# Overflow blocks, token sums and final norm moved into the block of the expert loop

## The reference

```python
x = x + g1 * mix
h2 = rmsnorm(x, norm2) * (1.0 + sc2) + sh2
ffn = moe(h2, ...)            # top 4 of 32 experts; 1024 -> 1024 (gate, up) -> 1024 (down)
x = x + g2 * ffn
y = rmsnorm(x, final_norm)
# moe: contrib = y_rows[dest] * g_s[:, None];  zeros_like(h).at[tok_s].add(contrib)
```

## Time and profile before

| | us |
|---|---|
| median of 3 runs | 1440.04 (1436.89 to 1440.72) |
| the profiled execution's own time | 1436.63 |
| its span | 1434.8 |
| PE busy | 1278.8 (89% of the span) |
| DVE, ACT, POOL busy | 459.5, 135.3, 282.2 |
| data moved by DMA | 479.23 MB, 334 GB/s over the span |

### The profile page before, as it was taken

How to read it: one execution, slowest core, us unless ns; L and a number is a source line. 1 busy time by engine, 2 the same in 40 slices (tenths; PEclk the granted TensorE clock), 3 DMA queues, 4 the chain that set the end, 5 groups by cost and what they waited for, 6 DMA issues and landing times. The chain is left out here.

```text
span 1434.8 us, 32026 instructions
## 1 busy us (share of the span) xinstructions
PE 1278.8 (89%) x13745; PEld 746.7 (52%) x13745; DVE 459.5 (32%) x676; ACT 135.3 (9%) x270; POOL 282.2 (20%) x335
## 2 busy tenths in 40 slices
PE   4999989566999999999999999999999999999710
PEld 2777634311356556655555665544545666566500
DVE  1210153452222333322223333222233333222244
ACT  3100101200000000100000000100000001000102
POOL 4002100152111111222111111221111112220126
PEclk9999989779999999999999999999999999999955
DMA  9736830625999999999999999999999999999161
GB/s 325 223 111 230 329 145 30 257 101 198 398 417 409 412 413 410 409 398 395 419 416 411 405 412 410 406 406 416 409 412 408 411 407 396 414 405 415 44 260 68
DMA packets 88787, 479.23 MB, mean 334 GB/s; under 512 B 15235, under 2 KB 24939, under 8 KB 39061
## 3 DMA queue, kind: packets, MB, share of 16 engines
q1 hardware_dynamic: 73842, 456.59, 79.5%
q0 software_dynamic: 11840, 20.64, 4.1%
q10 hardware_dynamic: 3075, 1.58, 0.5%
HBM read 468.41 MB, written 17.84 MB: 339 GB/s over the span
## 5 line engine op out<-in xcount | busy, mean ns | idle before, releaser
L1433 PE MATMUL acc<-raw_b,ht 128*32 128x512 f32 x3120 | 376.2, 597 | 16.2 <-DVE ht L1264 9.0
L1433 PE MATMUL acc<-raw,ht 128*32 128x512 f32 x3024 | 371.6, 596 | 12.5 <-DVE ht L1264 6.5
L1433 PEld LDWEIGHTS acc<-raw,ht 128*32 128x32 f32 x3024 | 168.7, 110 | 185.2 <-issue 155.4
L1433 PEld LDWEIGHTS acc<-raw_b,ht 128*32 128x32 f32 x3120 | 146.2, 110 | 220.7 <-issue 204.2
L1154 POOL DMA_INDIRECT rows<-h_rows,row_next x90 | 91.6, 1018 | 752.2 <-DVE row_next L1259 732.8
L1312 DVE TENSOR_TENSOR g_sb<-acc,bias_gu 128x768 f32<-128x768 f32 x32 | 30.7, 958 | 623.7 <-PE acc L1433 623.7
L1451 PE MATMUL acc<-raw,at 128*32 128x256 f32 x3168 | 198.2, 379 | 2.7 <-DVE at L1270 2.6
L1451 PE MATMUL acc<-raw_b,at 128*32 128x256 f32 x2976 | 186.9, 379 | 0.0
L1451 PEld LDWEIGHTS acc<-raw,at 128*32 128x32 f32 x3168 | 144.2, 109 | 37.1 <-DVE at L1270 3.1
L1451 PEld LDWEIGHTS acc<-raw_b,at 128*32 128x32 f32 x2976 | 138.2, 110 | 41.2 <-issue 8.3
L909 PE MATMUL acc<-h_t,raw 128*128 128x288 f32 (+1 forms) x512 | 118.4, 393 | 1.1 <-DVE h_t L670 1.1
(11 more groups left out here) (217 smaller groups left out, 546.1 us busy)
## 6 DMA issues: line engine op xcount, KB each, us to landing
raw<-in_w_down SPq DMA_DIRECT2D x66, 1024.0 KB, 9.0
raw_b<-in_w_gate SPq DMA_DIRECT2D x65, 1024.0 KB
raw_b<-in_w_up SPq DMA_DIRECT2D x65, 1024.0 KB
raw<-in_w_gate SPq DMA_DIRECT2D x63, 1024.0 KB, 7.0
raw<-in_w_up SPq DMA_DIRECT2D x63, 1024.0 KB, 9.3
raw_b<-in_w_down SPq DMA_DIRECT2D x62, 1024.0 KB
raw<-in_w_ada SPq DMA_DIRECT2D x24, 1024.0 KB, 11.7
raw<-in_w_in SPq DMA_DIRECT2D x8, 1024.0 KB, 13.8
```

What stands on the lines that cost most here:

```text
L1433: mm = pe.matmul(gu_ps[b][q * TB:(q + 1) * TB, :].rearrange("p (m n) -> p m n", m=2), ht[:, b, k, :], w[:, kk, :, q * CW:(q + 1) * CW], st ...
```

## The change

Blocks 2, 3 and 4 become one block, without the two barriers between them. Its parts:

- **Zero rows.** In block 1, ACT issues two DMAs after its last `leave` that write zeros over `y_dram` (2176 rows of 1024) and a new `late_dram` (640 rows), from a 1 KB row of zeros on each partition.
- **g2 early.** G2's rows are kept in `mod_g2`; PE spreads them into the transpose banks of PSUM right after `row_ids(1)`, and ACT copies them out (`g2_bc`, `g2_bc_s`), ahead of the gates' exponential.
- **Last three experts.** Experts 29 to 31 are no longer scattered to `y_dram`, but by an indirect DMA that adds, into `late_dram`, one row per token (`add_late`). Empty slots go to spill rows.
- **Token rows while the loop ends.** When the scatters of experts 0 to 28 are in `y_dram`, ACT fetches the tiles (`fetch`), and DVE sums each, times g2, into `x_sb` (`add_rows`). Rows of experts 29 to 31 read as zero there.
- **Last down projection.** It reads `ht` and writes the PSUM banks of gate, in place of `at` and the banks of down.
- **Overflow.** The skipped code stands behind the loop on every engine; a block would add to `late_dram`.
- **End.** SP fetches five tiles of 4 KB rows from `late_dram`; DVE multiplies by g2, adds to `x_sb`, inverts, and applies both scales in one instruction; ACT squares and roots. POOL does nothing there. The root's table is loaded earlier, by a dummy root.

```diff
+            act.wait_ge(pool_step, POOL_STEPS)
+            for dram in (y_dram, late_dram):
+                rows_ = dram.rearrange("r (q n) -> (r q) n", n=CW).rearrange("(p r) n -> p r n", p=P)
+                act.dma_start(rows_, zeros[:, :].unsqueeze(1).to_broadcast([P, rows_.shape[1], CW]))\
+                    .then_inc(rows_zeroed, 16)
...
+                def add_late(e):
+                    pool.wait_ge(late_set, LATE)
+                    pool.wait_ge(y_scaled, SB * (e + 1))
+                    pool.wait_ge(y_stored, 16 * SB * e)
+                    for b in range(SB):
+                        pool.indirect_dma_start(late_quarter,
+                                                bass.IndirectOffsetOnAxis(ap=late_idx[e - E + LATE][:, b:b + 1], axis=0),
+                                                y_sb[:, b, :], None, bounds_check=Q * NTOK + SB * P - 1, oob_is_err=True,
+                                                compute_op=ALU.add).then_inc(y_stored, 16)
...
-                step(E - 1)
-                scatter(E - 2)
-                scatter(E - 1)
+                for e in range(E - LATE, E):
+                    add_late(e)
+                pool.wait_ge(x_added, TT)
                 pool.wait_ge(y_stored, 16 * SB * E)
...
                 def sigmoid(e):
                     act.wait_ge(g_clipped, e + 1)
+                    if not (isinstance(e, int) and e == 0):
+                        act.wait_ge(at_ready, e)
...
+                def fetch(t):
+                    r = norm_rows(t)
+                    if t >= 2:
+                        act.wait_ge(x_added, t - 1)
+                    act.dma_start(picked[t % 2][0:r, :, :].rearrange("p k d -> p (k d)"),
+                                  y_dram[TOPK * P * t:TOPK * (P * t + r), :].rearrange("(p k) d -> p (k d)", k=TOPK))\
+                        .then_inc(picked_in[t % 2], 16)
+                act.wait_ge(g2_spread, 1)
+                act.activation(g2_bc[:, :], flat(tp[:, :, :]), ACT.Copy).then_inc(g2_copied, 1)
+                act.wait_ge(g2_spread, 2)
+                act.activation(g2_bc_s[:, :], flat(tp[:, :, :])[0:NS, :], ACT.Copy).then_inc(g2_copied, 1)
                 act.wait_ge(shifted, 1)
                 act.activation(gates[:, :, :], gates[:, :, :], ACT.Exp).then_inc(exp_done, 1)
...
-                step(E - 1)
+                act.wait_ge(y_stored, 16 * SB * (E - LATE))
+                fetch(0)
+                fetch(1)
+                y_out(E - 3)
+                fetch(2)
+                fetch(3)
+                sigmoid(E - 1)
+                fetch(PT)
                 y_out(E - 2)
+                act.wait_ge(fin_set, 2)
+                act.activation(warm[:, :], warm[:, :], ACT.Sqrt).then_inc(warmed, 1)
                 y_out(E - 1)
...
                 def turn_act(e):
                     dve.wait_ge(act_ready, e + 1)
+                    if isinstance(e, int) and e == E - 1:
+                        dve.transpose(ht[:, :, :, :], turned(a_sb)).then_inc(at_ready, 1)
+                        return
...
                     if not (isinstance(i, int) and i < 2):
                         y_add(i - 2, pos(i, 0))
+                    if last:
+                        add_rows(0)
+                        add_rows(1)
...
                 step(E - 1)
                 turn_act(E - 1)
+                add_rows(2)
                 y_add(E - 2, NCH * E - MCH)
                 down_bias(E - 1)
+                add_rows(3)
                 y_add(E - 1, TOTAL)
+                add_rows(4)
...
+                def last_rows(t):
+                    r = norm_rows(t)
+                    z = late[t][0:r, :]
+                    dve.wait_ge(late_in[t], 16)
+                    dve.tensor_tensor(z, z, g2_of(t), ALU.mult).then_inc(late_step, 1)
+                    dve.wait_ge(late_step, t + 1)
+                    dve.tensor_tensor(x_sb[0:r, t, :], x_sb[0:r, t, :], z, ALU.add).then_inc(x2_ready, 1)
+                def finish(t):
+                    r = norm_rows(t)
+                    dve.wait_ge(fin_sqrt, t + 1)
+                    dve.reciprocal(fin_rstd[0:r, t:t + 1], fin_ss[0:r, t:t + 1]).then_inc(fin_set, 1)
+                    dve.wait_ge(fin_set, 3 + t)
+                    if t == 0:
+                        dve.wait_ge(fn_loaded, 16)
+                    dve.scalar_tensor_tensor(out=late[t][0:r, :], in0=x_sb[0:r, t, :], scalar=fin_rstd[0:r, t:t + 1],
+                                             in1=fn_bc[0:r, :], op0=ALU.mult, op1=ALU.mult).then_inc(out_ready, 1)
+                for t in range(TT):
+                    last_rows(t)
+                    if t:
+                        finish(t - 1)
+                finish(TT - 1)
...
                 row_ids(0)
                 row_ids(1)
+                for n, (sel_, r) in enumerate(((sel_p, P), (sel_s, NS))):
+                    if n:
+                        pe.wait_ge(g2_copied, n)
+                    for q in range(Q):
+                        mm = pe.matmul(tp[0:r, q // 2, (q % 2) * QW:(q % 2 + 1) * QW], sel_[:, q, :],
+                                       mod_g2[:, :], start=True, stop=True)
+                    mm.then_inc(g2_spread, 1)
                 gate_up(0)
```

More of the change, by code:

```diff
@@ L1118, in at_e @@
                 return t[:, :, e:e + 1] if isinstance(e, int) else t[:, :, bass.ds(e, 1)]
+            LOADS = DENSE_CH // SLOTS
+            ov_rows, ov_ht, ov_at, ov_g = [picked[0][:, j, :] for j in range(TOPK)]
+            ov_s, ov_u, ov_y, ov_late = [picked[1][:, j, :] for j in range(TOPK)]
+            ov_bias = ring_b[:, 0:3 * D].rearrange("p (m d) -> p m d", m=3)
+            ov_member = sb("ov_member", [P, TT, P], BF16)
+            held = sb("ov_held", [P, TT, 5], BF16)
+            rest = sb("ov_rest", [P, TT, 1])
@@ new lines, in hybrid_step, with blocks @@
+            ov_summed = sem("ov_summed")
+            ov_done = sem("ov_done")
+            tp_flat, ov_g_ps, ov_u_ps, ov_y_ps = [flat(t[:, :, :]) for t in (tp, acc_g, acc_u, acc_y)]
+            def blocks(eng, body):
+                eng.wait_ge(ov_listed, 1)
+                n = eng.value_load(n_ov_i[0:1, 0:1], min_val=0, max_val=MAX_OV)
+                with eng.If(n > 0):
+                    with eng.Fori(0, MAX_OV) as j:
+                        with eng.If(j < n):
+                            body(j)
+                            eng.wait_ge(ov_done, 16 * j + 16)
+                            eng.nop(nofuse=True)
@@ L1120, in hybrid_step, with g2_of @@
+            late = [picked[t // TOPK][:, t % TOPK, :] for t in range(TT)]
+            square_out = picked[1][:, TOPK - 1, :]
+            def g2_of(t):
+                return (g2_bc if t < PT else g2_bc_s)[0:norm_rows(t), :]
             block2 = experts.enter_context(nc.Block())
@@ L1307, in step @@
                         ids_next(i + 1)
+                    if isinstance(i, int) and i == 1:
+                        for n in range(LATE):
+                            e = E - LATE + n
+                            dve.scalar_tensor_tensor(out=late_idx[n][:, :], in0=table[:, :, e, 0], scalar=q_col[:, 0:1],
+                                                     in1=spill_row[:, :], op0=ALU.add, op1=ALU.min).then_inc(late_set, 1)
                     if not (isinstance(i, int) and i < 2):
                         y_add(i - 2, pos(i, 0))
+                    if last:
+                        add_rows(0)
+                        add_rows(1)
                     dve.wait_ge(mm_done, pos(i, 2 * MCH - 1) + 1)
@@ L1628, in body @@
+                def body(j):
+                    pe.wait_ge(ov_member_ready, j + 1)
                     for t in range(TT):
-                        mm = pe.matmul(y_ps[:, 0:6], member[:, t, :], held[:, t, :], start=(t == 0),
+                        mm = pe.matmul(ov_y_ps[:, 0:5], ov_member[:, t, :], held[:, t, :], start=(t == 0),
                                        stop=(t == TT - 1))
```

495 lines of the change are left out of this document (209 added, 286 removed).

## The result

| | before | changed |
|---|---|---|
| median of 7 runs each, same chip | 1439.2 | 1430.05 (1423.75 to 1430.74) |
| ratio, 95% interval | | 0.993 (0.9909 to 0.995) |
| the profiled execution's own time, span | 1436.63, 1434.8 | 1430.74, 1429.0 |
| PE, DVE, ACT, POOL busy | 1278.8, 459.5, 135.3, 282.2 | 1286.6, 475.9, 133.8, 259.3 |
| moved by DMA | 479.23 MB | 493.34 MB |

A forecast was written before the change was run, and what follows sets the result against it. The prediction took PE at its pace in the expert loop as the bound; its terms, -2.6 + 1.7 - 8.05 - 35.45 + 4.8 + 1.5 = -38.1, took 1440.04 to 1402 us, with a range of 1395 to 1415.

The forecast's parts named there:

- Zero rows: ACT's zero writes from 172 us, 11,264 rows: cost 0 if issuing takes ACT under 3.96 us.
- Rival C: ACT held by the zero rows for 56 us from 172, delaying mix(0): 1447 us, slower than before; chance 0.05.
- Last down projection: Expert 31, loop's end: PE's 2.60 us wait for the transpose goes, saving 2.6 us.
- Bias add to last row in memory: Tail, from last bias add to last scatter's landing: +1.7 us net, with 1.2 for adding in memory.
- even race: Loop's end: expert 30's adding scatter lands at 1353.8, against PE's new end of 1354.2; 0.8 us allowed.
- Drain and block 3: Tail: POOL's drain, memset, count load and barrier, 8.85 us, shrink to 0.8, saving 8.05 us.
- The end: Final five tiles, fetch to last store: 61.15 us become 25.7, saving 35.45 us.
- g2 early: Ahead of gate_up(0): g2's spreads and copies before the gates' exponential delay PE, +4.8 us.
- Fetches beside the last weights: Last two experts: ACT's tile fetches make the last weights late, +1.5 us, bounds 0 and 7.
- B: Last two experts: the fetches starve PE or DVE, +8 us over the fetch term, 1410 us; chance 0.10.
- What bounds the kernel: Expert loop: PE at its pace, DMA with almost nothing left; what counts lies outside the unchanged loop body.

The follow-up runs named there:

- e6: e1 with PE's g2 spreads moved behind the first two gate and up projections; ratio 0.9788 to the kernel before.
- e7: e1 with the scatters of the last three experts writing instead of adding; 1411.1 us, ratio 0.9763 to the kernel before.
- e1: Changed kernel with ACT's two zero DMAs issued behind its copies of the mixer, not ahead of them; 1404.7 us, ratio 0.9753 to the kernel before.
- e8: e1 with the fetches of tiles 0 and 1 issued behind ACT's gates of expert 29 and the sums moved to suit; ratio 0.9796.
- e4: Changed kernel with the gates' exponential ahead of g2's two copies on ACT; 1422.3 us, ratio 0.9884 to the kernel before.
- e11: e10 with e8's later fetches and the sums of tiles 3 and 4 behind the last bias add; 1414.1 us, ratio 0.9764.
- e17: The kernel of e11 run again in a later group, on a chip of the first kind; ratio 0.9753 to the kernel before.
- e16: The kernel of e10 run again in a later group, on a chip of the first kind; ratio 0.9742 to the kernel before.
- e13: Changed kernel without an edit, on another chip (30.96 us an expert); 1397.5 us, ratio 1.0067 to the kernel before.
- e9: e5 with POOL's 20 scatters into the slot table issued only after gate_up(0); 1405.2 us, ratio 0.9703 to the kernel before.
- e12: Changed kernel with the edits of e1, e4, e9 and e10, on the chip of e13; 1382.7 us, ratio 0.9972 to the kernel before.
- e14: Kernel before the change with e9's wait for POOL's scatters, on the chip of e13; 1402.9 us, ratio 1.0116 to the kernel before.
- e10: e5 with one more dummy root on ACT behind the skipped overflow blocks; 1410.6 us, ratio 0.9738 to the kernel before.
- e5: Changed kernel with the edits of e1 and e4 together; 1413.0 us, ratio 0.976 to the kernel before.

## Why the prediction was wrong

**The step that failed** is *Zero rows*: "0, if issuing costs ACT under 3.96 us". The condition was the right one and I let it pass: issuing cost 33.3 us, and 21.5 of them reached PE (23.6 at `mix(0)`, 2.1 of which PE had lost before the zeros were issued). Rival C named the mechanism and the place, with 56 us of hold and a chance of 0.05; a hold of 33 costs 33.3 - 3.96 - 7.0 = 22.3 by its own working, so its partial form was the case. (By the same working the hold that uses up a gain of 38.1 is 49 us, and not the 45 of my text.) What I set against it was an issue of 0.37 us for 1,024 rows. That row says nothing here: it is the rows ahead on the queue that hold an issue and not its own, and this one had some 860 ahead. Other issues of the same weights in the same trace, at 28.18, 33.72 and 37.90, took 3.3 to 5.5 us, and would have told me so. The 2.1 us are chance: `mix(0)` starts at 185.9 in e6 and e7 and at 188.1 in e1 and e8, which are the same up to there.

**Last down projection**, -2.6: right, the wait is gone.

**Bias add to last row in memory**: forecast 9.7 us from PE's end (8.0 before, +1.7), measured 11.7 (1390.6 to 1402.3). The even race came out as forecast (the bias add waits for expert 30's landing, but starts 0.6 behind PE's end); adding costs 3.1 where I had 1.2, mostly in issues of up to 2.2 us which I had not priced. The rule that I weighed there (the Trainium skill, "DMA: Bandwidth & Descriptors", anatomy of one DMA, 2.0 us fixed) is nearer to the landing of an adding scatter, 2.15 us from the end of its issue, than my 1.2; a writing one took 1.2 before and 1.4 in e7.

**Drain and block 3**, -8.05: right within 0.3. SP's fetch follows the landing by 1.05 us; I had 0.8. The branch to distant code that the Trainium skill warns of ("Runtime: NRT & Kernel Launch", instruction fetch mechanics) cost nothing that this row shows.

**The end**, 25.7: measured 3.56 + 19.7 + 2.4 = 25.7. That it fits to the tenth is in part luck: the fetch took 0.7 more than forecast and DVE's part 0.7 less (3.8 us a tile; the parts of my 4.0, 2.5 + 0.16 + 1.5, add up to 4.2).

**g2 early**, +4.8: measured 4.3, and avoidable (e4). **Fetches beside the last weights**, +1.5: PE's waits are 3.9. Against e8, e11 and e17, where PE needs 20.7 us from expert 31's g_sb to its end, the changed kernel needs 5.9 more and e16 7.6 more (28.3), so the bound of 7 holds for the changed kernel on its chip and is passed in e16; on the chip of e13 it was 23. The rival to it, B, had 8 over the term: I had taken the weights to be 17 us early, which does not hold where they land 18 us behind their issue.

**What bounds the kernel**: "the loop is PE at its pace" was wrong in one way. PE is busy all through, but its own pace is 30.96 us an expert, and in the loop it needs 32.1 to 32.4. It isn't the loads alone that slow it: in every trace from these chips one interval, from expert 19's g_sb to expert 20's, is 30.96 (948.13 to 979.09 in the kernel before), and in the two traces compared here PE is busy all of it and the DMA engines stand at a share of 1.00 to 1.02, as in the intervals beside it. The 1.2 us, and the 2.1 to 5.7 us by which the stretch of the changed kernel and its variants (40.7 to 43.9, e9 apart) exceeds that of the kernel before (38.2 and 38.5), are put down to issue by the profile, on every chip but that of e12 to e14; that they have one cause is not shown. The stretch was no step of my sum (+3.3). What PE is short of stays open. The Trainium skill, "Runtime: NRT & Kernel Launch", section on instruction fetch mechanics, has the instructions refilled from memory in blocks of 16 KiB, and calls crossing into a new one mostly hidden. The traces show such blocks, as packets of kind "instruction" in part 3. None falls in the thin part of the kernel before (the nearest come at 304.7 and 335.2) or of the changed one (329.7 and 364.1); in e9 one does, at 346.6, and takes 1.0 us. Between 460 and 1340 in the kernel before there is none at all, and nearly every expert pays its 1.2 us. So refills don't explain the 1.2 us, and for the thin part no slow one shows.

In the traces, the changed kernel's -5.8 is made of +23.6 at `mix(0)`, -0.7 to the block's start, +4.3 for g2, +3.3 for the stretch, +1.2 in the loop, +2.2 in the last two projections (3.9 of waits for weights and 0.9 that the rows don't name, less 2.6), and -39.6 for the tail, 78.0 to 38.4, where I had forecast 36.2. Against the forecast of -38.1 that is 32.3 too much, and the hold is 21.5 of it.

## What to carry to other kernels

A DMA that is issued behind thousands of rows on the same queue stopped its engine's whole list here until most of them were moved: count the rows ahead, not bytes, keep a DMA of thousands of rows the last of its queue for a while, and put it behind what others wait for. Look at the longest issue of a line and not at one row of it. A gain at the end of a kernel is read against what the same edit puts at its head. And DMA slack has to be measured on more than one chip: 9 MB beside the last weights cost 4 to 8 us where an expert took 32.1 to 32.4 us and 23 where it took 31.0, most of what turned the whole change from a gain of 0.7% into a loss of 0.7%. The version with e1, e4, e9 and e10 (e12) is 0.3% under the kernel before on the chip where the change alone loses, and an estimated 1.4% without e9's wait. On the others that wait gains: 2.6% under the kernel before without it (e16), 3.0% with it (e9).

## What the runs showed of the hardware

- The hold: an issue on ACT's queue waited until the DMA ahead was down to 1,200 to 1,600 rows (four traces, rows of 1 and of 4 KB); over all runs the hold was 15.9 to 33.5 us; on SP's queue six waited 2.7 to 5.5 us, until 1,030 to 1,200 rows of all DMAs ahead were left, and none with under 1,050 ahead waited.
- After 5 to 9 us without work PE was granted 1.2 GHz in most of the first 6 us of `gate_up(0)` (32 to 36 matmuls recorded, five traces), after 0.6 to 2.2 us it was 2.4 GHz throughout (56, five traces: e4, e5, e9, e10, e12).
- An adding scatter of 128 rows of 1 KB took POOL 1.56 to 2.1 us to issue at the end of the changed kernel (up to 3.15 in other places and runs), a writing one 0.98 there in e7 (up to 1.8 elsewhere).
- Chips differ by 3.7 to 4.3% on the same kernel (1386 against 1439 to 1448): PE needs 31.0 us an expert on one and 32.1 to 32.4 on the others, and 23.5 against 41.5 us for the changed kernel's stretch. It is not the clock that is granted: 1.00 in the loop's stretches on both.
